# Griffin/RWKV-7 trunk with a hierarchical mixture of experts on one core: rows of the first two experts gathered in halves of k, sample rows scaled by ScalarE, second tile's router logits split in two

## The chip, the cores and the metric

The kernel runs on one core of a Trainium2 chip, as one program. The metric is the device time of one execution in microseconds (us). The core has TensorE (matmuls and, as PEld, the loads of their stationary operand), VectorE (DVE), ScalarE (ACT), GpSimd (POOL) and SyncE (SP), and 16 DMA engines. ACTq, SPq and POOLq in the rows are the parts of these engines that issue transfers.

## The reference, cut to what matters

The model is one layer over 256 prompt tokens and 64 sample tokens (320 in all, width 1024). After the two mixers and their output projection, a mixture of 32 experts in 4 groups follows:

```python
x = x + merged @ w_out
# _hier_moe(_rmsnorm(x, norm2), ...), t: 320 x 1024
pg = softmax(t @ rg + rgb)                      # 4 groups, the best one is taken
le = (t @ re + reb).reshape(-1, 4, 8)           # 8 experts of a group, the best two are taken
...
h = silu(einsum('nd,edf->nef', t, wg)) * einsum('nd,edf->nef', t, wu)   # 1024 -> 256
h = h * comb[:, :, None]
y = einsum('nef,efd->nd', h, wd)                # 256 -> 1024
```

All of it is float32. Each expert has 3 MB of weights (gate, up and down, 1 MB each), all 32 of which are read from HBM.

## The kernel before

The kernel has three stages. Up to about 494 us it computes the mixers in eight turns over pairs of heads. From there to about 553 us it computes the output projection, the second norm, the router and the places of the tokens. From 553 us it runs the 32 experts, each over a buffer of 64 token slots, and ends with a sum of the experts' outputs and the last norm. The waits between engines are semaphores written out by hand, and each engine's instructions stand in the order of its block in the code.

Tokens lie in three tiles: t = 0 and 1 with 128 prompt tokens each, t = 2 with the 64 sample tokens. Tile 2 is kept as two halves of the width, `x1h` and `xn2h`: partitions 0 to 63 hold columns 0 to 511 of the 64 rows, partitions 64 to 127 hold columns 512 to 1023.

**Norm and logits.** `out(t, k0, k1)` (the matmuls are at L1096) is the output projection. DVE adds the residual (L2013) and signals `x1r`. ACT squares and sums the row (`square`, L1542 and L1544), takes the root (`root`, L1551 and L1554), and DVE inverts it (`inverse`, L1990) and scales the rows (`plain`, L1995, signals `xn2`). TensorE transposes the unscaled rows (`x2`, L1107 and L1115), ACT copies them out as `xn2T` (`cols`, L1560 and L1565), and TensorE computes the logits of a tile (`logits`, L1140: 8 matmuls for tiles 0 and 1, 16 for tile 2). For tile 2 `both_halves` (L1122) adds the two halves' sums of squares. DVE scales the logits (L2004). ACT writes the normed rows to a scratch in HBM, `xn2d` (L1588 and L1591), from which GpSimd later gathers the rows of experts 2 and on (L681).

**The choice.** From `logits(2)` a chain of small DVE operations (L2030 to L2045) makes the mask `Mk`. TensorE counts with it (L1158 to L1163), and DVE builds `disp` (L2057), a one-hot matrix, token by slot, for experts 0 and 1. In between TensorE runs matmuls that nobody reads (`unread`, L770).

**Rows of the first two experts.** `disp` times `xn2` gives the 128 rows (2 experts x 64 slots) as two halves of the width, in banks 0 and 3. Each half takes three matmuls of 512 columns: two of L1170 (tiles 0 and 1, 128 partitions) and one of L1171 (tile 2, 64 partitions), and signals `rows_ps`. ACT copies each half to `xg01` (L1599, `rows_c`). TensorE waits for both copies and transposes chunk k out of the columns k, k+8, k+16 ... of `xg01` (L1175), eight in all. DVE multiplies them by the norm's gains in two halves (L2089, `gT`), and the first expert's gate and up matmuls (L1201) begin with k = 0 to 3. DVE then makes the list of tokens of the other experts (to L2084, then L2099 to L2104), after `places` on TensorE (L1185).

**The weights' queue.** SP issues the weight loads in an order of its own (L553, L556, L579, L583, L611). Where a buffer is still in use it waits first. Around this change it goes:

```python
sp.wait_ge(S("lg_ps"), 2)
load_dn(3, 3)
load_dn(4, 4, (2,))
sp.wait_ge(S("xn2d"), 64)
sp.wait_ge(S("rows_ps"), 2)
load_dn(2, 2)
load_dn(4, 4, (0,))
```

The loads behind `rows_ps` go into the memory of `xn2` (`wkv`), which L1170 and L1171 read. Behind them stand the other parts of experts 5 and 6 and then, each after its buffer comes free, experts 7 to 31.

Of the kernel before, what the change touches and what calls it, by code (L numbers as in the profile page):

```python
# [9 lines left out]
ACT = mybir.ActivationFunctionType  # L10
AX = mybir.AxisListType

P = 128
D = 1024
KC = D // P
# [150 lines left out]
def hawk_rwkv7_moe(nc, a, o):  # L166
    ctx = ExitStack()
    with ctx:
# [5 lines left out]
        def S(name):  # L174

            if name not in sems:
                sems[name] = ctx.enter_context(nc.semaphore("s_" + name))
            return sems[name]
# [139 lines left out]
        def at64(e):  # L318
            return slice(64 * e, 64 * e + 64)
# [410 lines left out]
        def _(pe):  # L730
# [369 lines left out]
            def x2(t):  # L1100

                n = TILES[t][1]
                pe.wait_ge(S("x1r"), t + 1)
                if t == 2:
                    pe.wait_ge(S("xn2T"), 3)
                    for c in range(4):
                        q = tr(bank[7][:, c * P:c * P + P], x1h[:, c * P:c * P + P], ident)  # L1107
                    q.then_inc(S("x2T_ps"), 1)
                    return
                for j in range(2):  # L1110
                    if t:
                        pe.wait_ge(S("xn2T"), 2 * t + j - 1)
                    for c in range(4):
                        d = (4 * j + c) * P
                        q = tr(bank[0 if j else 7][:, c * P:c * P + n], x1[0:n, t, d:d + P], ident[0:n, 0:n])  # L1115
                    q.then_inc(S("x2T_ps"), 1)

            def both_halves(n_sq):

                pe.wait_ge(S("sumsq"), n_sq)  # L1120
                for h in range(2):
                    q = mm(bank[1][at64(h), 0:1], C("i64"), rowst[:, 2:3], start=True, stop=True)  # L1122
                q.then_inc(S("sum2"), 1)
# [7 lines left out]
            q.then_inc(S("rowL_ps"), 1)  # L1131
            out(1, 0, KC)

            def logits(t):

                t0, n = TILES[t]
                pe.wait_ge(S("xn2T"), min(2 * t + 2, 5))
                for k in range(KC):
                    for r in ([slice(0, P)] if t < 2 else [at64(0), at64(1)]):
                        q = mm(bank[4 if t == 2 else 5][r, 64 * t:64 * t + NG + NE], xn2T[:, k, t0:t0 + n], rw[:, k, :], start=(k == 0), stop=(k == KC - 1))  # L1140
                return q
# [5 lines left out]
            pe.wait_ge(S("rw_n"), 1)  # L1147
            logits(0)
            out(2, 4, KC)
            logits(1).then_inc(S("lg_ps"), 1)  # L1150
            x2(2)
            both_halves(6)
            logits(2).then_inc(S("lg_ps"), 1)

# [9 lines left out]

            unread(bank[2][:], 1)
            pe.wait_ge(S("disp"), 1)
            for h in range(2):
                b, c = bank[3 if h else 0], slice(512 * h, 512 * h + 512)
                for t in range(2):
                    mm(b[:], disp[:, t].rearrange("p e s -> p (e s)"), xn2[:, t, c], start=(t == 0), stop=False)  # L1170
                mm(b[:], disp[at64(h), 2].rearrange("p e s -> p (e s)"), xn2h[at64(h), :], start=False, stop=True).then_inc(S("rows_ps"), 1)  # L1171
            pe.wait_ge(S("rows_c"), 2)
            for k in range(KC):
                c = P * (k % 4)
                q = tr(bank[1 if k < 4 else 4][:, c:c + P], xg01[:, k:D:KC], ident)  # L1175
                if k % 4 == 3:
                    q.then_inc(S("gT_ps"), 1)

# [154 lines left out]
        def _(act):  # L1333
# [252 lines left out]
            for t in range(2):  # L1586
                act.wait_ge(S("xn2"), t + 1)
                act.dma_start(xn2d[t * P:t * P + P, :], xn2[:, t, :]).then_inc(S("xn2d"), 16)  # L1588
            act.wait_ge(S("xn2"), 3)
            for h in range(2):  # L1590
                act.dma_start(xn2d[NPROMPT:N, 512 * h:512 * h + 512], xn2h[at64(h), :]).then_inc(S("xn2d"), 16)  # L1591
# [43 lines left out]
        def _(dve):  # L1635
# [351 lines left out]
            def inverse(t):  # L1987

                n = P if t == 2 else TILES[t][1]
                step(nc.vector.reciprocal(rowst[0:n, 6 + t:7 + t], rowst[0:n, 3 + t:4 + t]))  # L1990

            def plain(t):

                dst, x = (xn2h, x1h) if t == 2 else (xn2[:, t, :], x1[:, t, :])
                TS(dst, x, rowst[:, 6 + t:7 + t], None, MUL).then_inc(S("xn2"), 1)  # L1995

            def scale(t, gains, sem):

# [3 lines left out]
            def logits(t):  # L2002

                step(STT(lg[:, t, :], bank[4 if t == 2 else 5][:, 64 * t:64 * t + NG + NE], rowst[:, 6 + t:7 + t], rb[:], MUL, ADD))  # L2004
# [3 lines left out]
            for t in range(3):  # L2008
                dve.wait_ge(S("wo_ps"), t + 1 if t < 2 else 4)
                for h in range(2 if t < 2 else 1):  # L2010
                    c = slice(512 * h, 512 * h + 512)
                    x = x1[:, t, c] if t < 2 else x1h
                    q = TT(x, x, ob[2 * t + h][:], ADD)  # L2013
                q.then_inc(S("x1r"), 1)
                if t == 2:
                    dve.wait_ge(S("lg_ps"), 1)
                    logits(0)
                    logits(1)
                dve.wait_ge(S("rms"), 4 + t)
                inverse(t)  # L2020
                plain(t)
            dve.wait_ge(S("lg_ps"), 2)
            logits(2)

# [222 lines left out]
```

## Time and profile before

| | |
|---|---|
| time, median of 3 runs | 789.84 us (789.63 to 792.54) |
| the profiled execution | 789.78 us, of which the span is 788.0 us |
| granted TensorE clock, mean | 0.989 |
| TensorE matmul busy | 745.1 us (95%) |
| VectorE busy | 444.6 us (56%) |
| ScalarE busy | 238.7 us (30%) |
| read from HBM | 154.43 MB |

A row of the timeline has the start in us, the duration in us, the engine, the source line, the operation with its output and inputs, and in brackets the idle time before it and what ended it. A float32 matmul leaves two records (x2), a transpose one. The span begins with the first instruction of the profile, and the time has 1.8 us more.

### The profile page before, as it was taken

What the parts mean: (1) busy time and instruction counts of PE and PEld (TensorE: products, weight loads), DVE (VectorE), ACT (ScalarE), POOL (GpSimd) and SP (SyncE); (2) the same over time, 40 slices, a digit from 0 to 9 for tenths busy, and PEclk for the clock granted to TensorE, in tenths of its full rate; (3) what the DMA queues carried; (4) which work ended last, traced back from release to release, by engine and by line L of the source; (5) the groups of instructions that cost most, each with busy time, mean ns of one, the idle gap of its engine ahead of it and who ended that gap; (6) DMA issues with size and microseconds to landing.
All of it is one profiled execution on the core that took longest, in us unless ns stands there. A gap on an engine that the chain in (4) does not pass through costs nothing.

```text
span 788.0 us, 18161 instructions
## 1 busy us (share of the span) xinstructions
PE 745.1 (95%) x7060; PEld 464.0 (59%) x7060; DVE 444.6 (56%) x1172; ACT 238.7 (30%) x591; POOL 61.3 (8%) x71
## 2 busy tenths in 40 slices
PE   4999999999999999999999989999899999998884
PEld 4666666666666676666766665444555555554431
DVE  3365677777777767867867765416323432232226
ACT  4234443352451453444434433322000001000012
POOL 3000000400000000000000000000131222222100
PEclk9999999999999999999999999999999999999998
DMA  9344142780160251151341732896999999999965
GB/s 241 98 113 124 28 132 73 142 208 14 28 195 7 66 163 27 41 161 27 86 116 27 256 132 76 298 396 261 396 411 410 419 420 419 421 409 421 400 271 193
DMA packets 116838, 160.06 MB, mean 203 GB/s; under 512 B 27858, under 2 KB 92172, under 8 KB 110120
## 3 DMA queue, kind: packets, MB, share of 16 engines
q1 hardware_dynamic: 100244, 147.57, 52.3%
q0 software_dynamic: 5760, 7.80, 3.9%
q10 hardware_dynamic: 10789, 4.06, 2.0%
q8 instruction: 31, 0.51, 0.2%
q14 instruction: 14, 0.11, 0.0%
HBM read 154.43 MB, written 15.73 MB: 216 GB/s over the span
## 4 chain that ended last, share of the span: by engine, by line
PE 82%; DMA 8%; DVE 3%; SPq 3%; issue 1%; ACT 1%; POOL 0%; POOLq 0%; ACTq 0%; DVEq 0%
PE bank L790 24%; PE bank L1201 11%; PE bank L962 5%; PE bank L796 5%; PE bank L1096 4%; PE bank L1208 4%; PE bank L1040 4%; DMA vecs<-in_exp_up 2%; DMA shared<-in_exp_up 2%; PE bank L762 2%; PE bank L895 2%; PE bank L904 2%; PE bank L1230 1%; SPq L583 1%; PE bank L992 1%
## 5 line engine op out<-in xcount | busy, mean ns | idle before, releaser
L790 PE MATMUL bank<-xnT,wall 128*128 128x320 f32 x656 | 194.7, 441 | 0.0
L790 PEld LDWEIGHTS bank<-xnT,wall 128*128 128x128 f32 x656 | 118.6, 190 | 45.1 <-issue 2.6
L2148 DVE COPY vecs<-bank 128x512 f32<-128x512 f32 x32 | 22.1, 691 | 60.5 <-DMA ybuf<-vecs,sidx 32.8
L681 POOL DMA_INDIRECT merged<-xn2d,gidx x15 | 15.6, 1039 | 519.0 <-DVE gidx L2104 410.6
L2153 DVE TENSOR_TENSOR scratch<-bank,n 128x512 f32<-128x512 f32 x30 | 20.5, 688 | 49.3 <-PE bank L1201 45.7
L962 PE MATMUL bank<-xnT,wall 128*128 128x320 f32 x128 | 47.9, 456 | 0.3
L1201 PE MATMUL bank<-vecs,scratch 128*64 128x256 f32 x352 | 42.1, 394 | 4.1 <-DMA vecs<-in_exp_up 3.5
L1604 ACT ACTIVATE vecs<-bank 128x128 f32<-128x128 f32 x32 | 8.9, 278 | 119.5 <-PE bank L1201 119.5
L1201 PE MATMUL bank<-scratch 128*64 128x256 f32 x320 | 36.7, 382 | 1.9 <-DMA scratch<-in_exp_up 1.4
L1201 PEld LDWEIGHTS bank<-vecs,scratch 128*64 128x64 f32 x352 | 25.6, 141 | 17.1 <-DMA vecs<-in_exp_up 4.2
L1371 ACT ACTIVATE shared<-bank 128x256 f32<-128x256 f32 x32 | 12.3, 386 | 73.4 <-PE bank L790 66.7
L685 POOL DMA_INDIRECT ybuf<-vecs,sidx x30 | 30.1, 1002 | 48.7 <-DVE vecs L2148 36.1
L1040 PE MATMUL bank<-xnT,wall 128*128 128x320 f32 x112 | 33.1, 439 | 0.7
L1608 ACT ACTIVATE vecs<-bank 128x128 f32<-128x128 f32 x32 | 8.9, 278 | 74.6 <-PE bank L1237 74.6
L1096 PE MATMUL bank<-wall,merged 128*128 128x512 f32 (+1 forms) x84 | 30.9, 596 | 0.1
L1201 PEld LDWEIGHTS bank<-scratch 128*64 128x64 f32 x320 | 22.5, 137 | 12.9 <-DMA scratch<-in_exp_up 1.6
L2161 DVE SCALAR_TENSOR_TENSOR vecs<-vecs,bank 128x128 f32<-128x128 f32 x32 | 9.0, 283 | 36.7 <-ACT vecs L1604 36.6
L796 PE MATMUL bank<-vecs,consts_sb 128*128 128x320 f32 x64 | 24.7, 467 | 2.1 <-ACT vecs L1401 1.1
L1040 PEld LDWEIGHTS bank<-xnT,wall 128*128 128x128 f32 x112 | 20.7, 190 | 9.4 <-issue 1.4
L1477 ACT ACTIVATE wkv<-bank 64x128 f32<-64x128 f32 x32 | 8.7, 272 | 53.6 <-PE bank L992 42.6
L1908 DVE SCALAR_TENSOR_TENSOR wkv<-bank,shared,consts_sb 128x128 f32<-128x128 f32 x32 | 11.2, 351 | 19.8 <-PE bank L1002 19.8
L962 PEld LDWEIGHTS bank<-xnT,wall 128*128 128x128 f32 x128 | 19.3, 191 | 4.7 <-DVE wkv L1900 3.1
(426 smaller groups left out, 1358.6 us busy)
## 6 DMA issues: line engine op xcount, KB each, us to landing
wall<-in_w_in SPq DMA_DIRECT2D x58, 512.0 KB, 5.4
vecs<-in_exp_gate SPq DMA_DIRECT2D x11, 1024.0 KB, 10.7
vecs<-in_exp_up SPq DMA_DIRECT2D x11, 1024.0 KB, 13.2
scratch<-in_exp_gate SPq DMA_DIRECT2D x10, 1024.0 KB, 14.7
scratch<-in_exp_up SPq DMA_DIRECT2D x10, 1024.0 KB, 17.2
scratch<-in_exp_down SPq DMA_DIRECT2D x6, 1024.0 KB, 14.6
shared<-in_exp_gate SPq DMA_DIRECT2D x10, 512.0 KB, 15.7
shared<-in_exp_up SPq DMA_DIRECT2D x10, 512.0 KB, 18.4
```

Source lines behind the costliest of these rows:

```text
L685: pool.indirect_dma_start(yhalf, bass.IndirectOffsetOnAxis(ap=e, axis=0), ye[:, b, :], None, bounds_check=4 * QROWS - 1, oob_is_err=False) ...
L762: q = mm(bank[5 + j][0:w, 0:N], wbuf[n][:, k, 0:w], xnT[:, k, :], start=(k == 0), stop=(k == KC - 1))
L790: q = mm(tpbank(L, name), wbuf[name][:, k, :], xnT[:, k, :], start=(k == 0), stop=(k == KC - 1))
L796: mm(tpbank(L, name), lhsT, rhs, start=True, stop=True).then_inc(S("tp"), 1)
L895: q = mm(bank[2][r, 16 * u:16 * u + 16], am[r, u, e, 0, cols5(h)], lower(X[r, u:u + 1, :], k), start=True, stop=True)
L962: q = mm(tpbank(L, "gr"), wbuf["gr"][:, k, :], xnT[:, k, :], start=(k == 0), stop=(k == KC - 1))
L1040: q = mm(tpbank(L, "lx"), wbuf["lx"][:, k, :], xnT[:, k, :], start=(k == 0), stop=(k == KC - 1))
L1096: q = mm(b, merged[:, k, t0:t0 + n], wo[k][:, 512 * h:512 * h + 512], start=(k == 0), stop=(k == KC - 1))
L1201: q = mm(b[64 * f:64 * f + 64, 0:256], xT[:, k, :], gate_up(w, k)[:, :, 128 * f:128 * f + 128], start=(k == 0), stop=(k == KC - 1))
L1208: q = mm(b[64 * d:64 * d + 64, :], hT[:, 64 * j:64 * j + 64], down(w, j, d), start=(j == 0), stop=(j == 1))
L2148: CP(ye[:, e % 2, :], bank[6 + e % 2][:]).then_inc(S("ye"), 1)
L2153: TT(xgT[:, 0:2, 4 * j:4 * j + 4, :].rearrange("p b k s -> p k b s"), b[:].rearrange("p (k b s) -> p k b s", k=4, b=2), n2[:, 4 * j:4 * j ...
```

## The change

Four edits are made together.

1. `logits(1)` is split: k = 0 to 3 are issued before `x2(2)`, k = 4 to 7 behind it.
2. The sample rows `xn2h` are no longer scaled by DVE (`plain(2)`) but by ACT, behind its stores of tiles 0 and 1. DVE makes the reciprocal and signals `rstd2`. TensorE now waits for `xn2` >= 3 ahead of the rows.
3. The rows of the first two experts are computed in halves of k (k = 0 to 3, then 4 to 7) and no longer in halves of the width. The moving operand `xn2` is read in steps of 8 elements (32 bytes), 4 times 128 columns. A half takes four matmuls: tile 0 (512 columns), the first half of tile 2 (256 columns, 64 partitions), tile 1 (512 columns), and behind a wait for `rows_g0` the second half of tile 2 (256 columns, 64 partitions).
4. The first four transposes wait for the first copy alone, the next four for the second, and all read 128 neighbouring columns.

```diff
--- before.py
+++ after.py
@@ -1131,11 +1131,11 @@
             q.then_inc(S("rowL_ps"), 1)
             out(1, 0, KC)
 
-            def logits(t):
+            def logits(t, k0=0, k1=KC):
 
                 t0, n = TILES[t]
                 pe.wait_ge(S("xn2T"), min(2 * t + 2, 5))
-                for k in range(KC):
+                for k in range(k0, k1):
                     for r in ([slice(0, P)] if t < 2 else [at64(0), at64(1)]):
                         q = mm(bank[4 if t == 2 else 5][r, 64 * t:64 * t + NG + NE], xn2T[:, k, t0:t0 + n], rw[:, k, :], start=(k == 0), stop=(k == KC - 1))
                 return q
@@ -1147,8 +1147,9 @@
             pe.wait_ge(S("rw_n"), 1)
             logits(0)
             out(2, 4, KC)
-            logits(1).then_inc(S("lg_ps"), 1)
+            logits(1, 0, 4)
             x2(2)
+            logits(1, 4, KC).then_inc(S("lg_ps"), 1)
             both_halves(6)
             logits(2).then_inc(S("lg_ps"), 1)
 
@@ -1164,15 +1165,23 @@
 
             unread(bank[2][:], 1)
             pe.wait_ge(S("disp"), 1)
+            pe.wait_ge(S("xn2"), 3)
             for h in range(2):
-                b, c = bank[3 if h else 0], slice(512 * h, 512 * h + 512)
-                for t in range(2):
-                    mm(b[:], disp[:, t].rearrange("p e s -> p (e s)"), xn2[:, t, c], start=(t == 0), stop=False)
-                mm(b[:], disp[at64(h), 2].rearrange("p e s -> p (e s)"), xn2h[at64(h), :], start=False, stop=True).then_inc(S("rows_ps"), 1)
-            pe.wait_ge(S("rows_c"), 2)
+                b = bank[3 if h else 0][:].rearrange("s (k q) -> s k q", k=4)
+                for g in range(2):
+                    mm(b, disp[:, g].rearrange("p e s -> p (e s)"), xn2[:, g, :].rearrange("p (q k) -> p k q", k=KC)[:, 4 * h:4 * h + 4, :],
+                       start=(g == 0), stop=False, skip_group_check=True)
+                    if g:
+                        pe.wait_ge(S("rows_g0"), h + 1)
+                    q = mm(b[:, :, at64(g)], disp[at64(g), 2].rearrange("p e s -> p (e s)"),
+                           xn2h[at64(g), :].rearrange("p (q k) -> p k q", k=KC)[:, 4 * h:4 * h + 4, :],
+                           start=False, stop=(g == 1), skip_group_check=True)
+                    q.then_inc(S("rows_ps" if g else "rows_g0"), 1)
             for k in range(KC):
                 c = P * (k % 4)
-                q = tr(bank[1 if k < 4 else 4][:, c:c + P], xg01[:, k:D:KC], ident)
+                if k % 4 == 0:
+                    pe.wait_ge(S("rows_c"), k // 4 + 1)
+                q = tr(bank[1 if k < 4 else 4][:, c:c + P], xg01[:, P * k:P * k + P], ident)
                 if k % 4 == 3:
                     q.then_inc(S("gT_ps"), 1)
 
@@ -1586,6 +1595,8 @@
             for t in range(2):
                 act.wait_ge(S("xn2"), t + 1)
                 act.dma_start(xn2d[t * P:t * P + P, :], xn2[:, t, :]).then_inc(S("xn2d"), 16)
+            act.wait_ge(S("rstd2"), 1)
+            A(xn2h, x1h, ACT.Copy, scale=rowst[:, 8:9]).then_inc(S("xn2"), 1)
             act.wait_ge(S("xn2"), 3)
             for h in range(2):
                 act.dma_start(xn2d[NPROMPT:N, 512 * h:512 * h + 512], xn2h[at64(h), :]).then_inc(S("xn2d"), 16)
@@ -1991,8 +2002,7 @@
 
             def plain(t):
 
-                dst, x = (xn2h, x1h) if t == 2 else (xn2[:, t, :], x1[:, t, :])
-                TS(dst, x, rowst[:, 6 + t:7 + t], None, MUL).then_inc(S("xn2"), 1)
+                TS(xn2[:, t, :], x1[:, t, :], rowst[:, 6 + t:7 + t], None, MUL).then_inc(S("xn2"), 1)
 
             def scale(t, gains, sem):
 
@@ -2017,8 +2027,12 @@
                     logits(0)
                     logits(1)
                 dve.wait_ge(S("rms"), 4 + t)
-                inverse(t)
-                plain(t)
+                if t < 2:
+                    inverse(t)
+                    plain(t)
+                else:
+                    nc.vector.reciprocal(rowst[:, 8:9], rowst[:, 5:6]).then_inc(S("rstd2"), 1)
+                    dve.wait_ge(S("rstd2"), 1)
             dve.wait_ge(S("lg_ps"), 2)
             logits(2)
 
```

## Rows read from the trace of the kernel before

**Rows 1.** The page's shares: busy us of each engine.

```profile
PE 745.1 (95%) x7060; PEld 464.0 (59%) x7060; DVE 444.6 (56%) x1172; ACT 238.7 (30%) x591; POOL 61.3 (8%) x71
```

**Rows 2.** Busy time by stretch; last two columns: DMA share, GB/s.

```profile
546.00:547.00 1.00, 1.00 (x3) 0.29 (x2) 0.86 (x5) 0.00 (x0) 0.00 (x0) 1.00 0.77 297
547.00:548.00 1.00, 1.00 (x3) 0.25 (x2) 0.90 (x4) 0.14 (x1) 0.00 (x0) 1.00 0.08 31
...
550.00:551.00 1.00, 0.79 (x2) 0.00 (x0) 0.93 (x4) 0.18 (x1) 0.00 (x0) 1.00 0.00 0
...
553.00:755.00 202.00, 192.15 (x1398) 106.51 (x1400) 62.44 (x152) 17.74 (x62) 44.66 (x44) 0.99 1.02 415
```

**Rows 3.** What SP's queue waited for (total us, times, longest) and its issues.

```profile
SPq L605 <- PE bank L1171: 11.6, 1, 11.6
...
537.81 1.39 SPq L583 DMA_DIRECT2D xnT<-in_exp_down  x1
550.86 0.38 SPq L579 DMA_DIRECT2D wkv<-in_exp_down  x1
...
572.94 0.34 SPq L553 DMA_DIRECT2D scratch<-in_exp_gate  x1
```

**Rows 4.** The chain of waits that ended last: start us, us, what.

```profile
544.91 1.85 PE bank L1170 x4
546.77 1.05 PE bank L1171 x2
547.82 1.91 PE bank L1170 x4
549.73 1.07 PE bank L1171 x2
550.82 0.61 ACT merged L1599
...
559.94 7.60 DMA merged<-xn2d,gidx
...
753.18 5.26 PE bank L1201 x32
```

**Rows 5.** Timeline of PE, DVE, ACT and ACTq around the third tile.

```profile
533.09 1.97 PE L1140 MATMUL bank<-rw,xnT 128*128 128x36 f32 x16
534.90 0.64 PE L1107 MATMUL bank<-consts_sb,wkv 128*128 128x128 f32 x4
536.22 1.13 PE L1140 MATMUL bank<-rw,xnT 128*64 128x36 f32 x32 [0.47 <-ACT xnT L1560]
...
533.21 0.69 DVE L2013 TENSOR_TENSOR wkv<-wkv,bank 128x512 f32<-128x512 f32 x1 [7.01 <-PE bank L1096]
533.93 0.63 ACT L1542 ACTIVATE wkv<-wkv 128x512 f32<-128x512 f32 x1 [5.38 <-DVE wkv L2013]
535.57 0.60 ACT L1560 ACTIVATE xnT<-bank 128x512 f32<-128x512 f32 x1 [0.92 <-PE bank L1107]
536.62 0.48 DVE L1995 TENSOR_SCALAR wkv<-wkv,rowst 128x512 f32<-128x512 f32 x1
537.14 1.98 ACTq L1591 DMA_DIRECT2D xn2d<-wkv  x2
537.40 0.26 DVE L2004 SCALAR_TENSOR_TENSOR lg<-bank,rowst,rb 128x36 f32<-128x36 f32 x1 [0.29 <-PE bank L1140]
```

**Rows 6.** DMA issues: count, KB each, median us to landing.

```profile
xn2d<-wkv ACTq DMA_DIRECT2D x2, 128.0 KB, 9.1
```

**Rows 7.** Timeline: output projection, then transposes from neighbouring and from strided columns.

```profile
493.78 12.28 PE L1096 MATMUL bank<-wall,merged 128*128 128x512 f32 x28
...
522.23 1.04 PE L1115 MATMUL bank<-consts_sb,wkv 128*128 128x128 f32 x8
...
551.47 1.15 PE L1175 MATMUL bank<-consts_sb,merged 128*128 128x128 f32 x8 [0.69 <-ACT merged L1599]
```

**Rows 8.** Loads of the stationary operand for the same: ns min/median/max.

```profile
L1115 PEld LDWEIGHTS bank<-consts_sb,wkv x16: 138/140/143, 521.8 to 527.5; 128*128 128x128 f32 x16
L1175 PEld LDWEIGHTS bank<-consts_sb,merged x8: 186/188/207, 551.5 to 552.2; 128*128 128x128 f32 x8
```

## The prediction

> **What bounds the kernel now.** I read the page's shares first. TensorE is busy 95% of the span [rows 1], which looks like a kernel bound by TensorE. The table by stretch of time corrects this for the last third. From 553 to 755 us the DMA share is 1.02 at 415 GB/s [rows 2], while the same row still has ten us in which TensorE is idle. The share of one is the thing to see: all 16 DMA engines are full for 202 us, moving the experts' weights. The last of these weights lands at 753.18 us, and the gate and up matmuls that waited for them start at that moment in the chain [rows 4]. So behind 553 us the end is set by when the weight stream starts and how many bytes it has, not by how soon TensorE reaches an expert.
>
> Ahead of that stream the DMA engines are idle: share 0.77 in the stretch from 546 us, 0.08 in the next, 0.00 at 550 us [rows 2]. What ends the hole is read from SP's queue: it waited 11.6 us at L605 for the matmuls of L1171 (`rows_ps`), and issued the next load at 550.86 us, right behind the end of the second half's rows at about 550.8 us [rows 3, 4]. From there to full DMA engines it takes about 2 us. This is the place where the change touches the end: **each us by which `rows_ps` comes sooner or later moves the start of the stream, and with it the end, by one us.** All else at this place (the copy, the transposes, the first expert) is TensorE's path, and it matters only if the stream runs dry.
>
> **Edit 1, the split logits, and edit 2, the sample rows on ACT.** Today logits(1) starts at 533.09, x2(2) at 534.90, and logits(2) only at 536.22, 0.47 us of it idle until ACT has copied the transposed tile (535.57 + 0.60) [rows 5]. Half of logits(1) is (534.90 - 533.09) / 2 = 0.9 us. With the change the first half ends at 534.0; `x1r` is there, since DVE's sum ends at 533.21 + 0.69 = 533.90. The four transposes take about 0.5 us, to 534.5. ACT is still squaring until 533.93 + 0.63 and reads the accumulator after it, so its copy runs from about 534.85 to 535.45. Meanwhile TensorE does the second half of logits(1), to 535.4, then `both_halves`, 0.2 us, and starts logits(2) at about 535.7 instead of 536.22. That is 0.5 us sooner.
>
> DVE must follow. `lg_ps` for the first two tiles now comes at about 535.6 and not at 535.1, and two scalings of 0.26 us each take it to 536.2; root and reciprocal come at about 536.4. Were `plain(2)` still on DVE (0.48 us [rows 5]) it would end at 536.9, just as logits(2) does, so edit 2 is cover for edit 1 and earns little alone. On ACT it costs about 0.6 us, as the square of the same 128 x 512 does. Behind it on ACT stand the stores of L1591, now about 0.3 us later than 537.14, and a table load with two exponentials that wait for DVE long after. The stores land 9.1 us after issue [rows 6], which is about 547 to 549 us. SP waits for these too (`xn2d`), some 2 us before it needs them, so this is hidden; with an earlier `rows_ps` by more than 2 us it would be the next bound. TensorE's new wait for `xn2` >= 3 is met at about 537.4, seven us before the rows. Sum of edits 1 and 2 on the path to `disp`: **-0.5 us**, through the DVE chain, which has no other input. Between -0.6 (the whole wait gone and the copy with it) and 0 (the copy is not sooner, since ACT does it behind the square).
>
> SP's loads behind `lg_ps`, issued up to 537.81 + 1.39 [rows 3], come 0.5 us sooner as well. They only join the queue ahead of the hole and move its beginning, not its end: nothing.
>
> **Edit 3, the rows.** This is on the path that sets the end. Today the six matmuls take 1.85 + 1.05 + 1.91 + 1.07 = 5.88 us [rows 4], twelve records. The number of columns does not change: 2 x (512 + 512 + 512) then, 2 x (512 + 256 + 512 + 256) now. Two costs are new.
>
> *More changes of shape.* At the pace of the output projection, 12.28 / 28 = 0.44 us a record [rows 7], twelve records are 5.26 us; 0.62 us is over. I put it on the places where a 128-partition matmul follows a 64-partition one or the other way, since there the loads of the stationary operand start together with the matmul: four in the block, 0.155 us each. The new order has eight. That adds 4 x 0.155 = **0.62 us**; at least 0, if the time is not in the changes but in the bytes. The wait for `rows_g0` costs nothing: it is for a matmul that ends while the 512 columns behind it (0.85 us) are running, and only the last quarter of the half is queued behind it.
>
> *A strided moving operand.* No row of this kernel shows a moving operand read in steps of 32 bytes. The nearest is the stationary operand with the same step: eight transposes of L1175 take 1.15 us, eight from neighbouring columns 1.04 us [rows 7], and one load is 188 ns against 140 ns [rows 8]. The block reads 12 x 4 = 48 such pieces of 128 columns. By the difference of the groups, 0.11 / 8 = 0.014 us a piece, this is **0.66 us**. By the single loads it is 48 x 0.048 = 2.3 us, and 0 if a float32 matmul, which takes 2 cycles a column in each record, has room for it. I take 0.66, as the row that has both operands running, and keep 0 and 2.3 as bounds.
>
> The Trainium skill speaks against this edit: "SBUF — State Buffer", section "Door 1: The DMA port swizzle", says that consecutive reads in the same 16-byte line go at full speed and that each step to a new line pays a penalty, so a float32 step of 8 elements always pays. It gives no size; the trace agrees as far as its strided loads of the stationary operand are longer, and no row shows it for the moving one. What it could make of the time is rival C.
>
> **Edit 4, the halves.** Today TensorE waits 0.69 us for the second copy before the first transpose [rows 7]. Afterwards the first copy lies under the second half's matmuls, so this goes, and the transposes read neighbouring columns, 0.05 us for the first four. DVE is free for the gains only when its list of places is through, about 551.6 - 0.5, which holds the gain to about 0.5 us when the rows come late. The first expert starts some 0.5 us sooner relative to the rows. But this ends on TensorE's path, which has the full DMA engines behind it: the gather of experts 2 and 3 takes 7.60 us to land under that load [rows 4]. Price on the end: **0**. The cover is the stock of issued weights; SP's next load behind them is at 572.94 us [rows 3], and there is no gap in the DMA share around it.
>
> **Sum.** -0.5 + 0.62 + 0.66 + 0 = +0.8 us. The profiled execution took 789.78 us (788.0 of span and 1.8 around it), 0.06 under the median. 789.8 + 0.8 = **790.6 us**.
>
> **The rivals.**
> - A, the forecast: the release of the weight stream decides. From the bounds, -0.6 to -0.5 + 0.62 + 2.3 = +2.4: 789.2 to 792.2 us. For it: the hole ends at L1171 and the share of 1.02 for 202 us behind it. Chance 0.70.
> - B, TensorE's path decides: the stream has small gaps that a sooner first expert fills, and the rows are cheap. Then -0.5 - 0.69 + 0.2 = -1.0: 788.8 us. Against it: the chain of waits does name TensorE's matmuls for much of the stage, but the DMA share is full under them. Chance 0.14.
> - C, the other side: the strided moving operand goes at half pace. It adds the 5.3 us of the twelve records once more to the rows' block, all of it in the hole, so -0.5 + 0.62 + 5.3 = +5.4: 795.2 us. It decides from 1.7 times the pace on, where the sum passes +4.0 us. Against it: the stationary operand with this step loads 1.34 times as long, not twice. The Trainium skill's rule on lines would allow it ("each access that crosses to a new line pays a penalty"); no run here shows the size. Chance 0.09.
> - D, faster by over 4 us: `rows_ps` would have to come when the hole begins, and the stores of `xn2d` would not be down. Nothing in the edits reaches it. Chance 0.03.
> - E, the edits cancel at their cheap bounds, strided reads and changes of shape free, and only noise of a run is seen: 789.3 us. Chance 0.04.
>
> **How the numbers follow.** A measurement of this kernel tells about 0.5%, 3.95 us, from no change; its three runs already span 2.9 us. Within this are A, B and E: 0.88. Slower is C with 0.09, faster is D with 0.03. The range leaves out C and D and takes in A and B, with the spread of a median at either end: 788.2 to 793.0 us.
>
> **What would show it.** Right: SP's first load behind L605 at about 551.6 us (550.86 before); the rows' block 7.2 us long instead of 5.9; `disp` 0.5 us sooner, at about 544.3; no wait of 0.69 us ahead of the transposes; the first experts' matmuls within 0.5 us of 553.1; the DMA share at 1 from then to about 756 us. Wrong: a record of L1170 well over 0.6 us with 512 columns (C), the end moving while the first load stays (B), or a gap of the DMA engines behind 560 us.

## The result and the profile after

The changed kernel takes 797.0 us (median of 9 runs, 794.37 to 800.01) against 789.84 us of the kernel before (9 runs, 788.21 to 792.54). The ratio is 1.0084, 95% interval 1.0065 to 1.0103: 0.84% slower, some 7 us. The forecast was 790.6 us, "within 0.5%" with 0.88. What came was in kind rival C, which had 0.09.

The profiled execution took 797.17 us, of which 795.3 us are the span. The timeline of TensorE around the change, in the changed kernel (L1172 and L1176 are the rows' matmuls, L1184 the transposes, L1210 an expert's gate and up; they answer to L1170, L1171, L1175 and L1201 of before):

```profile
532.87 1.08 PE L1140 MATMUL bank<-rw,xnT 128*128 128x36 f32 x8
533.78 0.64 PE L1107 MATMUL bank<-consts_sb,wkv 128*128 128x128 f32 x4
534.25 0.98 PE L1140 MATMUL bank<-rw,xnT 128*128 128x36 f32 x8
535.16 0.28 PE L1122 MATMUL bank<-rowst,consts_sb 128*64 128x1 f32 x4
535.30 1.11 PE L1140 MATMUL bank<-rw,xnT 128*64 128x36 f32 x32
...
543.91 2.08 PE L1172 MATMUL bank<-wkv 128*128 128x512 f32 x2
545.92 1.16 PE L1176 MATMUL bank<-wkv 64*128 64x256 f32 x2
547.01 2.08 PE L1172 MATMUL bank<-wkv 128*128 128x512 f32 x2
549.02 1.26 PE L1176 MATMUL bank<-wkv 64*128 64x256 f32 x2
550.21 2.19 PE L1172 MATMUL bank<-wkv 128*128 128x512 f32 x2
552.33 1.27 PE L1176 MATMUL bank<-wkv 64*128 64x256 f32 x2
553.52 2.19 PE L1172 MATMUL bank<-wkv 128*128 128x512 f32 x2
555.64 1.26 PE L1176 MATMUL bank<-wkv 64*128 64x256 f32 x2
556.84 1.97 PE L1184 MATMUL bank<-consts_sb,merged 128*128 128x128 f32 x8
558.89 5.04 PE L1210 MATMUL bank<-vecs,scratch 128*64 128x256 f32 x32
563.75 1.24 PE L1194 MATMUL bank<-merged 128*64 128x41 f32 x24
564.92 3.67 PE L1210 MATMUL bank<-vecs,scratch 128*64 128x256 f32 x32
```

One matmul of 512 columns (x2) fills 2 us and one of 256 columns 1.1 us. Before, two matmuls of 512 columns together filled 1.85 us [rows 4]. From the first of them to the transposes it is 12.9 us (543.91 to 556.84); before it was 6.7 us (544.78 to 551.47), of which 0.69 us were the wait. The upper five rows are edit 1 at work: logits(2) starts at 535.30 with no wait ahead of it. The wait of 0.69 us ahead of the transposes is gone too. Yet these transposes take 1.97 us (1.15 before [rows 7]) and the first expert 5.04 us, where the second takes 3.67. The table by stretch says why. Its columns behind POOL are the granted clock, the DMA share and GB/s:

```profile
546.00:552.00 6.00, 6.00 (x8) 1.51 (x8) 4.31 (x15) 0.60 (x1) 0.00 (x0) 0.67 0.15 56
552.00:558.00 6.00, 6.00 (x13) 2.62 (x13) 0.01 (x1) 0.60 (x1) 0.00 (x0) 0.50 0.00 0
558.00:561.50 3.50, 3.42 (x17) 2.10 (x17) 2.67 (x9) 0.00 (x0) 0.00 (x0) 0.50 0.92 329
561.50:565.00 3.50, 3.50 (x48) 2.70 (x46) 0.00 (x0) 0.28 (x1) 0.00 (x0) 0.97 1.03 397
...
571.00:572.00 1.00, 0.57 (x5) 0.30 (x5) 0.90 (x3) 0.28 (x1) 0.00 (x0) 1.00 0.88 242
572.00:573.00 1.00, 1.00 (x6) 0.33 (x6) 0.00 (x0) 0.00 (x0) 0.00 (x0) 1.00 0.74 307
```

Some 4 us into the new matmuls the clock falls to half (0.50, 1.2 GHz), though the profile shows TensorE as busy in every us, and it stays there until about 561.6 us. The DMA share has a hole from 547 to 558 us, and another, small one at 571 to 573 us that the kernel before did not have. SP's queue, the waits and the issues:

```profile
SPq L605 <- PE bank L1176: 19.4, 1, 19.4
...
556.98 0.38 SPq L579 DMA_DIRECT2D wkv<-in_exp_down  x1
...
563.96 0.33 SPq L553 DMA_DIRECT2D vecs<-in_exp_gate  x1
```

The first load behind `rows_ps` goes out at 556.98 us, 6.12 us later than the 550.86 before [rows 3]. At the far end, the gate and up matmuls of expert 30, the last but one, start when their weights are in, at 761.22 us (753.18 before [rows 4]):

```profile
743.35 17.83 DMA shared<-in_exp_up
761.18 0.04 issue
761.22 3.67 PE bank L1210 x32
```

**Where the 7.3 us of the span lie.** The rows start 0.87 us sooner (543.91 instead of 544.78): 0.22 us of this were there before the edits come in (`logits(1)` starts at 532.87 instead of 533.09), and 0.70 us are edit 1. From there to SP's first load it is 13.07 us instead of 6.08: +6.99. From that load to the weights of expert 30 it is 204.24 us instead of 202.32: +1.92. From there to the end 34.1 instead of 34.8: -0.7. The sum is +7.3.

The second of these intervals, from SP's first `wkv` load behind L605 to the start of expert 30's matmuls, is called the stream below. It is a good yardstick, because everything ahead of it, which moves by 5 us between profiled runs of nearly the same code (the rows start at 543.2 us in one and at 548.3 us in another), falls out. This difference is there already where the output projection begins, and goes with the granted clock ahead of it: the projection begins at 491.65 us in x13, which had 1.00 in the first 50 us and from 450 to 494 us, and at 497.26 us in x9, which had 0.93 and 0.96 there.

### The profile page after: what moved, and what is told of

It reads as the page before. It is cut to its first block, busy times and chain, and to the rows that moved or that the text cites. A ratio compares the mean times of both kernels' runs of the same rounds, so it can differ in the third digit from the quotient of the medians.

```text
span 795.3 us, 18171 instructions
## 1 busy us (share of the span) xinstructions
PE 753.6 (95%) x7064; PEld 466.4 (59%) x7064; DVE 443.8 (56%) x1171; ACT 239.3 (30%) x592; POOL 61.3 (8%) x71
## 4 chain that ended last, share of the span: by engine, by line
PE 82%; DMA 8%; SPq 3%; DVE 3%; issue 1%; ACT 1%; POOL 0%; POOLq 0%; DVEq 0%; ACTq 0%
PE bank L790 24%; PE bank L1210 10%; PE bank L962 5%; PE bank L796 5%; PE bank L1217 4%; PE bank L1096 4%; PE bank L1040 4%; DMA shared<-in_exp_up 2%; DMA vecs<-in_exp_up 2%; PE bank L762 2%; PE bank L895 2%; PE bank L904 2%; PE bank L1239 1%; PE bank L992 1%; PE bank L824 1%
## 5 line engine op out<-in xcount | busy, mean ns | idle before, releaser
L1210 PE MATMUL bank<-vecs,scratch 128*64 128x256 f32 x352 | 43.5, 403 | 6.4 <-DMA vecs<-in_exp_up 6.3
L1210 PE MATMUL bank<-scratch 128*64 128x256 f32 x320 | 38.4, 395 | 3.3 <-DMA scratch<-in_exp_up 2.9
L1210 PEld LDWEIGHTS bank<-vecs,scratch 128*64 128x64 f32 x352 | 26.1, 145 | 20.5 <-DMA vecs<-in_exp_up 6.9
L1210 PEld LDWEIGHTS bank<-scratch 128*64 128x64 f32 x320 | 23.3, 141 | 15.3 <-DMA scratch<-in_exp_up 3.3
```

What stands on the lines that cost most here:

```text
L1210: q = mm(b[64 * f:64 * f + 64, 0:256], xT[:, k, :], gate_up(w, k)[:, :, 128 * f:128 * f + 128], start=(k == 0), stop=(k == KC - 1))
```

## The experiments

Fourteen runs in four lots, each lot with the kernel before on the same chip. "Rows" is from the rows' first matmul to SP's first load, "stream" as above, and "expert 7" is from SP's first load to its first load for expert 7, which waits for the first expert's matmuls. These three are from one profile of each run; the ratio is to the kernel before.

| run | median us | ratio (95%) | rows us | expert 7 us | stream us |
|---|---|---|---|---|---|
| before | 789.84 | | 6.08 | 5.97 | 202.32 |
| changed | 797.0 | 1.0084 (1.0065 to 1.0103) | 13.07 | 6.98 | 204.24 |
| x1_contig | 790.31 | 1.0004 (0.9987 to 1.0022) | 6.87 | 5.16 | 202.26 |
| x2_logits_act | 789.08 | 1.0000 (0.9982 to 1.0018) | 6.08 | 5.97 | 202.59 |
| x3_rows_only | 799.55 | 1.0130 (1.0107 to 1.0154) | 13.08 | 7.26 | 203.77 |
| x4_late_rows | 795.85 | 1.0076 (1.0055 to 1.0098) | 5.97 | 5.97 | 202.31 |
| x5_step4 | 794.48 | one run | 12.75 | 6.40 | 202.55 |
| x6_step2 | 791.99 | one run | 7.11 | 5.15 | 202.24 |
| x7_stored_by_k | 790.5 | 1.0002 (0.9981 to 1.0024) | 6.87 | 5.16 | 202.45 |
| x8_half_mb_ahead | 790.02 | 1.0017 (0.9990 to 1.0043) | 6.08 | 5.96 | 202.25 |
| x9_first_expert_1us | 792.15 | 1.0014 (0.9992 to 1.0036) | 6.08 | 7.12 | 204.48 |
| x10_first_expert_3us | 793.47 | 1.0035 (1.0012 to 1.0059) | 6.09 | 8.83 | 206.94 |
| x11_changed_again | 797.42 | 1.0084 (1.0054 to 1.0114) | 13.08 | 6.89 | 203.76 |
| x12_rows_only_again | 798.31 | 1.0091 (1.0065 to 1.0118) | 13.07 | 7.22 | 203.64 |
| x13_by_k_and_half_mb | 789.06 | 1.0000 (0.9983 to 1.0018) | 6.87 | 5.16 | 201.32 |
| x14_edits12_and_half_mb | 788.87 | 0.9977 (0.9956 to 0.9997) | 6.08 | 5.96 | 202.62 |

Where all the loads stand behind `rows_ps` (all runs but x8, x13 and x14), the stream is 202.2 to 202.6 us long as long as expert 7's load goes out 6.4 us or less behind the first one, and 203.6 us and more from 6.9 us on.

### Is it the step of the moving operand? (x1_contig)

```diff
-                    mm(b, disp[:, g].rearrange("p e s -> p (e s)"), xn2[:, g, :].rearrange("p (q k) -> p k q", k=KC)[:, 4 * h:4 * h + 4, :],
+                    mm(b, disp[:, g].rearrange("p e s -> p (e s)"), xn2[:, g, 512 * h:512 * h + 512].rearrange("p (k q) -> p k q", k=4),
...
-                           xn2h[at64(g), :].rearrange("p (q k) -> p k q", k=KC)[:, 4 * h:4 * h + 4, :],
+                           xn2h[at64(g), 256 * h:256 * h + 256].rearrange("p (k q) -> p k q", k=4),
```

> The changed kernel with the moving operand of the rows' matmuls read from neighbouring columns: same instructions, shapes, order and waits. It leaves out the regrouping by k, so the rows of the first two experts hold their columns in the wrong places. Theory S (the 32-byte step of the moving operand is the cost): the eight matmuls take 6.0 to 6.6 us instead of 12.8, the clock stays at full speed, the first load behind L605 is issued at about 550.3 instead of 557.0, and the time is 789.5 us or a little under, 0.9 to 1.0% under the changed kernel. Rival C (the eight changes between 128 and 64 partitions and the wait for rows_g0 are the cost): the block stays above 10 us and the time within 1 us of 797.

Theory S holds. The timeline of this run:

```profile
546.43 1.12 PE L1172 MATMUL bank<-wkv 128*128 128x512 f32 x2
547.49 0.70 PE L1176 MATMUL bank<-wkv 64*128 64x256 f32 x2
548.11 1.13 PE L1172 MATMUL bank<-wkv 128*128 128x512 f32 x2
...
553.16 1.41 PE L1184 MATMUL bank<-consts_sb,merged 128*128 128x128 f32 x8
```

The same eight matmuls, shapes and waits take 6.73 us to the transposes and not 12.9, a pair of 512 and 256 columns 1.68 us and not 3.10, and the granted clock is 1.00 throughout. The time is that of the kernel before. Rival C of this run, the changes of shape with the wait for `rows_g0`, is left with 6.87 - 6.08 = 0.79 us. It is the changes: the pairs of matmuls that hold the wait take 1.68 us from start to start, as those without it. The expected 550.3 us for the first load was missed (553.30), since everything ahead was 2.5 us later in this execution, which the row of 546.43 shows; the length of the block is what tells.

This run also moves `rows_ps` without moving the first expert. Counted from the start of the rows, SP's first load is 0.79 us later than before and the first expert's matmuls are where they were (8.32 us, 8.34 before), and expert 30's matmuls come 0.73 us later (209.13 us, 208.40 before; x7, with the same block, has 209.32). So a late `rows_ps` alone is passed on to the end of the stream.

### How far a step is free (x6_step2, x5_step4)

Steps of 2 and of 4 elements in place of 8; the edit is the view of the moving operand, for the step of 4:

```diff
-                    mm(b, disp[:, g].rearrange("p e s -> p (e s)"), xn2[:, g, :].rearrange("p (q k) -> p k q", k=KC)[:, 4 * h:4 * h + 4, :],
+                    mm(b, disp[:, g].rearrange("p e s -> p (e s)"), xn2[:, g, 512 * h:512 * h + 512].rearrange("p (q k) -> p k q", k=4),
```

> The same with a step of 2 elements (8 bytes), two reads in each 16-byte line; the regrouping is left out here too. If the cost is paid per 16-byte line and is hidden by a second read in it, a pair takes 1.68 us as from neighbouring columns and the block 6.7 us. If any step above one element costs, it is near 3.1 us a pair.

> The changed kernel with the moving operand read in steps of 4 elements (16 bytes) and not of 8, same shapes; the rows' columns end up in the wrong places, so the regrouping by k is left out. If each new 16-byte line costs the same, however far the step, a pair of 512 and 256 columns takes 3.1 us as with 8 elements and the block 12 to 13 us. If the cost grows with the distance, it is clearly under 3.1 us, between that and the 1.68 us of neighbouring columns.

First the timeline with a step of 2, then with a step of 4:

```profile
545.74 1.17 PE L1172 MATMUL bank<-wkv 128*128 128x512 f32 x2
546.83 0.71 PE L1176 MATMUL bank<-wkv 64*128 64x256 f32 x2
547.48 1.17 PE L1172 MATMUL bank<-wkv 128*128 128x512 f32 x2
```

```profile
543.18 2.05 PE L1172 MATMUL bank<-wkv 128*128 128x512 f32 x2
545.16 1.15 PE L1176 MATMUL bank<-wkv 64*128 64x256 f32 x2
546.23 2.04 PE L1172 MATMUL bank<-wkv 128*128 128x512 f32 x2
```

Start to start a pair is 1.68 us with neighbouring elements, 1.74 with a step of 2, 3.05 with a step of 4 and 3.10 with 8. The cost does not grow with the distance: it comes at once, between 8 and 16 bytes. This is the rule of the Trainium skill that the prediction named ("SBUF — State Buffer", section "Door 1: The DMA port swizzle": two reads in a line of 16 bytes are needed for full speed). The trace agrees with it. The size here, for a float32 moving operand, is 1.42 us on 768 columns, a factor of 1.85 on the pair.

The step of 4 also brought the clock to half (0.50 in its stretch from 552 to 558 us), the step of 2 did not (1.00). Each of the two steps has one run.

### The other two edits, alone and left out (x2_logits_act, x3_rows_only)

x2 puts the split of the logits and the scaling on ScalarE into the kernel before; x3 takes just these two out of the changed kernel. Core of x2:

```diff
-            logits(1).then_inc(S("lg_ps"), 1)
+            logits(1, 0, 4)
             x2(2)
+            logits(1, 4, KC).then_inc(S("lg_ps"), 1)
...
+            act.wait_ge(S("rstd2"), 1)
+            A(xn2h, x1h, ACT.Copy, scale=rowst[:, 8:9]).then_inc(S("xn2"), 1)
```

> The kernel before with edits 1 and 2 alone (split logits, sample rows on ScalarE). If the start of the weight stream sets the end, disp and rows_ps come 0.9 us sooner, as they did in the changed kernel up to disp, and the time falls by 0.9 us to about 788.9. If TensorE's path through the experts decides, the same 0.9 us shows too, so this run tells only whether these edits keep their gain; if they cost something (ScalarE, the later stores of the sample rows), it is 789.8 or more.

> The kernel before with edits 3 and 4 alone (rows in halves of k, strided moving operand). Theory S: rows_ps comes 0.9 us later than in the changed kernel, so the time is 797 + 0.9 = 797.9 us, and the whole loss of about 8 us is in these edits. If edits 1 and 2 have a part in the loss (stores of the sample rows later, ScalarE busy), it is below 797.

x2 is the same as before within 0.18%, so a gain of 0.5 to 0.9 us can be neither shown nor excluded by the time. Nothing was lost by these edits. The timeline shows the gain: from the start of `logits(1)` to that of `logits(2)` it is 2.43 us in x2 (533.28 to 535.71) and 3.13 us before. x3 has all of the loss. Its first ratio, 1.013, was 3 us more than it should have been beside the changed kernel, so both went once more onto one chip:

> The changed kernel once more, beside the run with edits 3 and 4 alone on the same chip. The first comparison has a ratio of 1.0084 to the kernel before, and the same is expected.

> Edits 3 and 4 alone once more. Its rows_ps is 0.6 us later than that of the changed kernel by the profiles, so it should be 0.6 to 1.0 us slower than the changed kernel on the same chip. The first time it had 1.013 of the kernel before, 3 us more than that. If the 3 us stay, edits 1 and 2 are worth more with the strided rows than alone; if not, it is the spread of one chip and day.

797.42 and 798.31 us: 0.9 us apart, which is in the expected range, though not clear of noise (the intervals of the two ratios overlap). The 3 us were spread, which is worth knowing of a median of six runs of this kernel. The start of the rows is no measure of edits 1 and 2 here: in this pair it is 546.07 us with them and 545.48 without. And in the profiles of both x3 and x12 the granted clock was also at half ahead of the rows (0.50 from 537 to 538 us, where the kernel before has 1.00), and `logits(2)` and the rows are 9.48 us apart instead of 8.56. x10 has such a fall too (0.50 from 538 to 541 us) with none of the edits, so it is not put down to them.

### How much comes from the start of the stream alone (x4_late_rows)

```diff
-            unread(bank[2][:], 1)
+            unread(bank[2][:], 8)
             pe.wait_ge(S("disp"), 1)
```

> The kernel before with seven more unread matmuls of 512 neighbouring columns ahead of the rows, which makes rows_ps about 6.0 us later while TensorE keeps its full clock. Theory R (the release of the weight stream sets the end, one us for one us): +6.0 us, 795.8. Theory K (part of the loss of 7.2 us is the half clock of 548 to 561.6 us, which makes the first expert slow, and so SP's next loads late): this run shows the +6.0 alone and the changed kernel 1 us or more over it. If TensorE's path or the stream has slack, less than +5.

SP's first load goes out at 556.85 us, almost where the changed kernel has it (556.98), with the clock at full speed. The time is 6.0 us over before by the ratio (1.0076), and the stream is 202.31 us long, as before. So a start of the rows that is 6.0 us later is 6.0 us at the end. This run delays all of TensorE's path together with `rows_ps`, so it doesn't say which of the two counts; x1 shows it for `rows_ps`, x9 and x10 below for the first expert. The changed kernel has the same start and a stream of 204.24, 203.76 in its second run; without edits 1 and 2 it is 203.77 and 203.64. This is 1.3 to 1.9 us more than a late start explains. It is seen in the profiles alone: by time the changed kernel is over x4 by 0.08% (1.0084 against 1.0076), well inside the intervals. Their timelines differ in the first expert: 5.04 us at half clock in the changed kernel, and SP's loads for expert 7 go out at 563.96, here at 562.82:

```profile
556.85 0.38 SPq L579 DMA_DIRECT2D wkv<-in_exp_down  x1
...
562.82 0.33 SPq L553 DMA_DIRECT2D vecs<-in_exp_gate  x1
```

### Does a later first expert cost anything? (x9_first_expert_1us, x10_first_expert_3us)

Two or four unread matmuls between the transposes and the first expert, `rows_ps` as before:

```diff
+            unread(bank[2][:], 2)
```

> The kernel before with two unread matmuls of 512 columns between the transposes and the first expert: rows_ps stays where it is, and the first expert and all that TensorE does behind it come about 1.2 us later. Theory R with stock (the prediction: enough weights are issued ahead, TensorE's path costs nothing): no change. Theory K (SP's next loads wait for the experts' matmuls and the stock just lasts, so the half clock over the first expert in the changed kernel costs its own us): +0.5 to +1.2 us.

> The same with four unread matmuls, which is about 2.9 us. Theory R: no change. Theory K: +1.5 to +2.9 us, and the DMA share shows a dip where the loads issued behind rows_ps are through and those behind the first expert's matmuls are not yet there.

The stock theory, which was mine in the prediction, falls. The first expert comes 1.15 and 2.87 us later, counted from the start of the rows, and the stream grows from 202.3 to 204.5 and 206.9 us. By time it is 0.14% (not clear of zero) and 0.35% (clear of it), 1.1 and 2.8 us. With four matmuls the table by stretch shows the place:

```profile
560.00:561.00 1.00, 1.00 (x14) 0.64 (x12) 0.00 (x0) 0.00 (x0) 0.00 (x0) 1.00 1.03 391
561.00:562.00 1.00, 1.00 (x18) 0.73 (x16) 0.00 (x0) 0.16 (x1) 0.00 (x0) 1.00 0.15 57
562.00:563.00 1.00, 1.00 (x19) 0.83 (x20) 0.10 (x1) 0.12 (x1) 0.00 (x0) 1.00 0.55 82
...
576.00:577.00 1.00, 1.00 (x8) 0.70 (x6) 0.00 (x0) 0.00 (x0) 0.27 (x1) 0.50 1.04 426
...
580.00:581.00 1.00, 1.00 (x10) 0.78 (x7) 0.32 (x2) 0.28 (x1) 0.00 (x0) 1.00 0.51 189
```

The loads issued right behind `rows_ps` are through at 561 us, and the next ones wait in SP's queue for the first expert's matmuls (issue at 561.83). A second dip follows at 580 us, ahead of the loads for expert 9. It has a cause of its own: from 575 to 579 us this execution had half the clock, expert 2's matmuls took 5.36 us instead of 3.67, and expert 9's loads, which go out right behind them, were late. So part of the 4.6 us of this stream is not due to the four matmuls; how much is open. x9 has one dip (0.39 from 563 to 564 us) and no fall of the clock, but why its stream grows by 2.2 us for a delay of 1.15 is open too. The kernel before has no dip: its share is 0.95 or more in every us from 553 to 575, with expert 7's loads out at 556.83 us. A delay of 1.15 us is enough to open one, so its queue holds hardly more than it needs.

### Two ways to a better kernel (x7, x8, x13, x14)

x7 keeps all edits and stores `xn2` and the scratch rows grouped by k when they are scaled, so that every matmul and transpose reads neighbouring columns:

```diff
-                TS(xn2[:, t, :], x1[:, t, :], rowst[:, 6 + t:7 + t], None, MUL).then_inc(S("xn2"), 1)
+                TS(xn2[:, t, :].rearrange("p (k q) -> p k q", k=KC), x1[:, t, :].rearrange("p (q k) -> p k q", k=KC), rowst[:, 6 + t:7 + t], None, MUL).then_inc(S("xn2"), 1)
...
-                    q = tr(bank[k // 4][:, c:c + P], xg[p % 2][:, k:D:KC], ident)
+                    q = tr(bank[k // 4][:, c:c + P], xg[p % 2][:, P * k:P * k + P], ident)
```

> All four edits, but xn2 is stored grouped by k when it is scaled (VectorE and ScalarE read x1 in steps of 8 and write neighbouring columns), the scratch in HBM holds the rows in that order too, and all transposes of gathered rows read neighbouring columns. The moving operand of the rows' matmuls is contiguous. Theory: the block takes 6.7 us as in the run with neighbouring columns, with disp 0.5 to 0.9 us sooner than before, so rows_ps within 0.3 us of before and the time within 1 us of 789.4; the eight transposes of a pair of experts fall from 1.08 to 0.87 us, hidden under the weight stream. Rival: the strided read costs VectorE and ScalarE as it costs TensorE (0.75 us would become 1.5), or the stores of the sample rows in pieces of 256 bytes land late (over 9.1 us) and hold SP's queue; then it is 1 us or more over 789.4.

Its time is that of before (1.0002), as the theory had it. The profile has `logits(2)` 0.70 us sooner behind `logits(1)` and the rows' block 0.79 us longer, so SP's first load stays where it was, within 0.15 us (17.92 us behind the start of `logits(1)`, 17.77 before); the first expert is 0.81 us nearer to SP's first load (1.45 us instead of 2.26), and the stream is no shorter for it (202.45). The rival was right in part: the strided reads do cost VectorE and ScalarE, but less than the double, and the stores of the sample rows land after 9.6 us (9.1 before [rows 6]), some 3 us ahead of SP's first load. Of the two lines of this run, the first is VectorE's (0.75 us without the step), the second ScalarE's (0.72 us in the changed kernel):

```profile
L2005 DVE TENSOR_SCALAR wkv<-wkv,rowst x2: 1149/1156/1162, 514.1 to 527.4; 128x1024 f32<-128x1024 f32 x2
...
L1599 ACT ACTIVATE wkv<-wkv,rowst x1: 1217/1217/1217, 538.6 to 538.6; 128x512 f32<-128x512 f32 x1
```

A read in steps of 32 bytes costs these engines 1.5 and 1.7 times the time, but off the path that sets the end: from `logits(2)` to the rows it is 8.62 us, as in x2.

x8 moves two loads that need no `rows_ps` ahead of SP's wait for it:

```diff
+            sp.wait_ge(S("rows_out"), 128)
+            for d in range(2):
+                sp.dma_start(once_dn[2 + d], a["exp_down"][0, RING, P:2 * P, 512 * d:512 * d + 512]).then_inc(S("ew6"), 16)
             sp.wait_ge(S("xn2d"), 64)
             sp.wait_ge(S("rows_ps"), 2)
             load_dn(2, 2)
```

> The kernel before with the two loads of 256 KB for expert 6 (rtb, lasts), which need no rows_ps, issued ahead of SP's wait for it. They fill part of the hole in the weight stream. Theory R (the stream's start and its bytes set the end): 0.52 MB at 415 GB/s is 1.26 us less behind rows_ps, 788.1 us. If TensorE's path through the experts sets the end, no change: 789.4 us.

No change: the stream is 202.25 us with 0.52 MB less in it. Its DMA engines drop to 184 GB/s from 557 to 558 us, since the loads behind `rows_ps` are now nearly through when those for expert 7 are issued. This is the place of the hole in x10, reached from the other side. What the dip leaves unmoved from 557 to 559 us is worth about 0.7 us at 415 GB/s, an estimate from these rows; where the rest of the 1.26 us went isn't shown.

> Stored by k as in the run of that name, and the two loads of 256 KB ahead of the wait for rows_ps. If the end is set by both the stream and TensorE's path, each move alone gives nothing and the two together do: by the run stored by k the first expert starts 1.45 us behind SP's first load and not 2.26, and 0.52 MB less lies behind it (1.26 us), so 0.8 to 1.2 us are gained: 788.8 us beside a kernel before of 789.8. If only the stream's start counts, no gain: 789.8.

> Edits 1 and 2 with the rows as before, and the same two loads ahead. Both the start of the stream and the first expert are 0.5 to 0.9 us sooner, but the stock behind rows_ps is 0.52 MB less, so the stream should run dry ahead of the loads for expert 7, as in the run with the half MB alone: a gain of 0.5 us at most, 789.3 us or the same as before.

By the stream both came out as expected: 201.32 us with both moves, the first 1.0 us gained by any run, and 202.62 us without the sooner first expert. The time can't tell. x13 has 1.0000 (0.9983 to 1.0018), and the 0.9987 that was expected lies inside the interval, as does no change. x14 has 0.9977 (0.9956 to 0.9997), just clear of 1, and the 0.9994 that was expected lies inside it too. So no version is shown to beat the kernel before by more than a few tenths of a per cent.

## Why the prediction was wrong

- **What sets the end** was right for `rows_ps`: it decides when the weight stream starts, and a delay there is passed on (x1: 0.79 us, 0.73 at expert 30; x4, with TensorE's path delayed as well: 6.0 us for 6.0). It held TensorE's path to be free unless the stream runs dry, and saw no gap. The stream does run dry at a delay of little over 1 us on that path (x9).
- **Edits 1 and 2** were right in kind and better than forecast: `logits(2)` comes 0.70 us sooner behind `logits(1)` in every profile with the edits (2.43 or 2.44 us instead of 3.13), against 0.5, and past the bound of 0.6; from there to the rows it is 8.6 us with and without them, at full clock. DVE was ready for logits(2) when it came, as foreseen. ScalarE's operation took 0.72 us.
- **Edit 3, more changes of shape:** 0.62 us forecast, 0.79 measured (x1), and the wait for `rows_g0` costs nothing, as forecast.
- **Edit 3, "A strided moving operand": this is the step that failed.** It said 0.66 us, with bounds of 0 and 2.3. Measured were 13.07 - 6.87 = 6.2 us, of which 4 x 1.42 = 5.7 are the reads at full clock and the rest their second half at half clock. The reasoning took the nearest row, transposes with a strided *stationary* operand, and its bounds from that operand too. But in those rows the longer loads of the stationary operand were partly hidden behind a moving one that was contiguous (8 x 0.048 = 0.38 us of them cost 0.11), and nothing said that the moving operand loses no more. No row of the trace bounded it from above, so the upper end should have come from a slower pace of every column, which is rival C. It was costed well (+5.4 us for the double pace, 1.85 measured) and given 0.09. The page of the Trainium skill that spoke against the edit ("SBUF — State Buffer", the section named above) had stated a rule that the trace could not refute, and the runs agree with it (3.05 us with a step of 16 bytes, 1.74 with 8). A rule of this kind deserves more than a tenth when the only contrary evidence is a row of another operand.
- **Edit 4, "Price on the end: 0", with the stock as cover:** wrong as well, and smaller. The share of 1 behind 553 us was read as a full queue, and "SP's next load behind them is at 572.94 us" was a misreading. That is expert 9's load; the next one behind those of `rows_ps` is expert 7's, 3.35 us after the last of them:

```profile
553.48 0.48 SPq L611 DMA_DIRECT2D lasts<-in_exp_down  x1
556.83 0.33 SPq L553 DMA_DIRECT2D vecs<-in_exp_gate  x1
```

  x9, x10 and x8 show the close fit: the loads behind `rows_ps` last just until the first expert has freed the next buffer. By itself the edit gained more than forecast (the first expert 0.81 us nearer to SP's first load in x1 and x7, against 0.5). In the changed kernel the half clock makes transposes and first expert some 2 us longer, and the stream is 1.3 to 1.9 us longer. That the one causes the other rests on x9, where a later first expert alone lengthens the stream, and on x5: there the clock fell to half too, but the first expert took only 4.45 us, expert 7's load was 0.43 us late (6.40 us) and not 1.01, and the stream stayed at 202.55 us. The clock was not varied by itself.
- **The clock** was not in the prediction at all, and no rival had it.
- **"The last of these weights lands at 753.18"** was a misreading: these are expert 30's, expert 31's come 7.8 us later. The chain goes through expert 30 because its matmuls stand ahead of `dn(29)`, whose rows are scattered last. It changed no number.

## What to carry to other kernels

Regroup a float32 operand where it is written, off the critical path, and not where TensorE streams it: a moving operand in steps of 16 bytes or more ran at about half pace here, one in steps of 8 bytes did not. Where a chain of loads behind one semaphore is in step with the engine that frees the next buffers, a DMA share of 1 proves no stock; put a short delay into the engine's path and see whether the end moves. And when a new access pattern has no row in the trace, the upper bound is what the worst stated rule would do, not the neighbour's price.

## What the hardware showed beside this

- The granted clock fell to 0.50 some 4 us after the first strided matmul, though TensorE was busy by the table in every us of that time (6.00 of 6.00), and rose again at about 561.6 us, in the middle of the first expert, 4.8 us after the contiguous transposes had begun. In the four other profiles with a step of 16 or 32 bytes it fell 4 to 6 us after the first strided matmul. The strided matmul of 512 columns hardly noticed: 2.08 us at full and 2.19 us at half clock. The contiguous work behind it did: 421 ns for one transpose against 273 in x1, and 5.04 us for the first expert against 3.67.
- With neighbouring elements and with a step of 2 the clock stayed at 1.00 through the same block, with steps of 4 and 8 it fell. So here it fell beside a slow moving operand, and not beside idle time that the profile shows. Slow moving operands are not its only occasion: in x3, x10 and x12 it fell for 3 to 4 us ahead of the rows as well, without one.
- Late in the kernel, where TensorE waits about 2 us for each expert's weights, some experts take 5.36 us and others 3.67 in one and the same execution, and which ones do changes from run to run. It is the clock: in the kernel before, the expert that starts at 722.07 us takes 5.36 us with a granted clock of 0.57 from 722 to 726 us, and the next one 3.67 us at 1.00. The spread of 5 us in the start of the rows lies ahead of all this.
